# Six single-pass filler products taken out of the routing and the first expert of a decoder step

## What is computed

```python
def moe_ffn(x, router_w, router_b, w_gu, b_gu, w_down, b_down):
    logits = x2.astype(jnp.float32) @ router_w.astype(jnp.float32) + router_b.astype(jnp.float32)
    top_vals, top_idx = lax.top_k(logits, TOP_K)
    gates = jax.nn.softmax(top_vals, axis=-1).astype(x.dtype)
    ...
    def expert_block(args):
        xb, e = args
        gu = xb @ w_gu[e] + b_gu[e]
        gate = jnp.minimum(gu[:, :D_FF], SWIGLU_LIMIT)
        up = jnp.clip(gu[:, D_FF:], -SWIGLU_LIMIT, SWIGLU_LIMIT)
        h = (up + 1.0) * (gate * jax.nn.sigmoid(SWIGLU_ALPHA * gate))
        return h @ w_down[e] + b_down[e]
```

## Time and profile before

| | us |
|---|---|
| median of 3 runs | 1199.98 |
| lowest, highest | 1198.43, 1200.36 |
| profiled execution, its own time | 1200.14 |
| its span | 1198.4 |
| PE busy | 1145.1 (96%) |
| VectorE (DVE) busy | 520.2 (43%) |
| ScalarE (ACT) busy | 259.7 (22%) |
| mean bandwidth | 370 GB/s |
| mean granted clock of TensorE | 0.992 |

### The profile page before, as it was taken

The page is one execution under the profiler, slowest core; times in us unless marked ns, Lnnn a source line. Parts: engine busy times, 40 slices in busy tenths (PEclk is TensorE's granted clock), DMA queues, the critical chain, the costliest instruction groups (busy, mean ns, idle before and its releaser), DMA issues.

```text
span 1198.4 us, 13942 instructions
## 1 busy us (share of the span) xinstructions
PE 1145.1 (96%) x5682; PEld 555.7 (46%) x5682; DVE 520.2 (43%) x989; ACT 259.7 (22%) x405; POOL 3.3 (0%) x13
## 2 busy tenths in 40 slices
PE   9999999999999999999999989999999999999994
PEld 8999999663333333333333323333333333333331
DVE  6788888882332223333233322322222222222236
ACT  4655655411111111111111111111111111111112
POOL 1000000000000000000000000000000000000000
PEclk9999999999999999999999999999999999999997
DMA  9865844768999999999999999999999999999994
GB/s 229 259 209 173 246 141 129 296 263 325 417 429 427 427 427 428 428 427 428 428 428 427 427 428 428 427 427 428 427 428 427 427 428 428 427 428 428 427 424 157
DMA packets 93276, 443.77 MB, mean 370 GB/s; under 512 B 7848, under 2 KB 65336, under 8 KB 67998
## 3 DMA queue, kind: packets, MB, share of 16 engines
q1 hardware_dynamic: 93038, 442.41, 91.4%
q10 hardware_dynamic: 176, 0.48, 0.1%
HBM read 441.34 MB, written 1.53 MB: 370 GB/s over the span
## 4 chain that ended last, share of the span: by engine, by line
PE 61%; DMA 29%; DVE 6%; ACT 2%; issue 1%; DVEq 0%; SPq 0%; ACTq 0%
DMA ring<-in_w_gu 24%; PE PS L914 21%; PE PS L954 14%; PE PS L705 10%; PE PS L822 6%; DMA ring<-in_w_down 3%; PE PS L844 3%; PE PS L726 2%; DVE w_lo L1060 1%; PE PS L830 1%; DVE tiles L1103 1%; PE PS L837 1%; PE PS L736 1%; PE PS L994 1%; PE PS L877 1%
## 5 line engine op out<-in xcount | busy, mean ns | idle before, releaser
L914 PE MATMUL PS<-ring,mid 128*64 128x512 f32 x1920 | 423.1, 594 | 25.1 <-DMA ring<-in_w_gu 24.6
L914 PEld LDWEIGHTS PS<-ring,mid 128*64 128x64 f32 x1920 | 135.3, 137 | 306.2 <-issue 254.2
L954 PE MATMUL PS<-ring,mid 128*64 128x512 f32 x960 | 213.1, 595 | 0.0
L1382 DVE TENSOR_SCALAR PS<-PS 128x512 f32<-128x512 f32 x30 | 21.0, 699 | 359.0 <-PE PS L914 359.0
L705 PE MATMUL PS<-x_hi,w_hi 128*128 128x320 f32 x448 | 141.2, 315 | 1.4 <-ACT tiles L523 0.6
L705 PE MATMUL PS<-x_lo,w_hi 128*128 128x320 f32 x448 | 139.0, 310 | 0.0
L705 PE MATMUL PS<-x_hi,w_lo 128*128 128x320 f32 x448 | 138.9, 310 | 0.0
L1364 DVE TENSOR_TENSOR ys<-PS,ys 64x512 fp32r<-64x512 f32 x64 | 44.1, 689 | 193.8 <-ACT ys L610 185.6
L954 PEld LDWEIGHTS PS<-ring,mid 128*64 128x64 f32 x960 | 66.1, 137 | 130.2 <-issue 130.0
L1103 DVE SCALAR_TENSOR_TENSOR x_tok<-PS,gate,x_tok 128x1024 f32<-128x1024 f32 (+1 forms) x93 | 115.1, 1276 | 21.0 <-PE PS L844 21.0
L601 ACT ACTIVATE mid<-PS 128x512 f32<-128x512 f32 x30 | 17.9, 597 | 424.7 <-DVE PS L1382 424.7
(11 more groups left out here) (241 smaller groups left out, 751.2 us busy)
## 6 DMA issues: line engine op xcount, KB each, us to landing
ring<-in_w_gu SPq DMA_DIRECT2D x125, 2048.0 KB, 40.3
ring<-in_w_down SPq DMA_DIRECT2D x62, 2048.0 KB, 38.8
raw<-in_w_in SPq DMA_DIRECT2D x56, 512.0 KB, 5.7
ring<-in_w_gu SPq DMA_DIRECT2D x6, 1024.0 KB, 7.9
ring<-in_w_out SPq DMA_DIRECT2D x4, 1024.0 KB, 5.3
ring<-in_w_down SPq DMA_DIRECT2D x4, 1024.0 KB, 41.5
x_tok<-in_x_prompt SPq DMA_DIRECT2D x2, 512.0 KB, 5.0
out<-x SPq DMA_DIRECT2D x2, 512.0 KB, 2.7
```

The costliest lines, as they stand in the source:

```text
L914: last = mm(PS[64 * a:64 * a + 64, b, :], xgT[:, 2 * (u % 2) + j, u // 2, :], w[:, o:o + HALF], start=False, stop=(u == 3 and j == 1))
L954: last = mm(PS[64 * a:64 * a + 64, XB, :], hT[:, j, u, :], w[:, j * D + a * HALF:j * D + (a + 1) * HALF], start=(u == 0 and j == 0), stop= ...
L1382: dve.tensor_scalar(gm, gm, LIMIT, None, ALU.min).then_inc(gm_ok, 1)
```

## The change

The six calls' products are removed, and with them the function that issued them. Everything else is as it was: the same waits in the same order, the same banks, the same transfers.

```diff
@@ -653,11 +653,6 @@
             mm = pe.matmul
 
-            def keep_warm(n, bank):
-
-                for _ in range(n):
-                    mm(PS[:, bank, :], ones_r[:, :], bias4[:, 0, :], start=True, stop=True)
-
             def keep_busy(n, bank):
@@ -801,7 +796,6 @@
             last.then_inc(so_turned, 1)
-            keep_warm(1, 1)
 
             pe.wait_ge(mask_ok, 1)
@@ -811,7 +805,6 @@
             last.then_inc(cnt_done, 1)
-            keep_warm(3, 1)
             pe.wait_ge(so_ok, 1)
@@ -901,7 +894,6 @@
                     turn_x(xg_sb, tx_done)
-                    keep_warm(2, 7)
                 pe.wait_ge(xgT_ok, 2 * it + rows_in(i))
```

## The result

| | before, us | changed, us |
|---|---|---|
| median of 14 runs | 1199.57 | 1201.07 |
| lowest, highest | 1198.43, 1200.61 | 1199.77, 1206.00 |
| profiled execution, its span | 1200.14, 1198.4 | 1201.13, 1199.4 |

The account below looks back on a forecast made before the run. The end was taken to hang on the weights' DMA stream, whose start waits for the first freed slots. 1200.14 - 0.09 + 1.41 = 1201.46; against the median, 0.16 lower, 1201.3 us; range 1198.3 to 1203.5.

Parts of the forecast that it names:

- The bound: Whole kernel: the end is that of the weights' DMA stream plus a short tail; TensorE waits for weights from about 650 us.
- Shifts the end by that microsecond: Between router and 296 us: each microsecond TensorE loses or gains shifts the whole stream and the end equally.
- One lost after 650 us would cost nothing: Late experts: TensorE already waits for weights there, so a microsecond it loses costs 0.
- The direct part: Routing: time gained by removing six filler products, apart from the clock; -0.09 us, far bound -1.6 us.
- Gain: 0.09 us, not 0.78: Three fillers ahead of the gather: it also needs VectorE's one-hot matrix, so it starts at about 266.72 instead of 266.81.
- the other two places: Fillers ahead of the mask product and ahead of the expert's first products: hidden in waits, gain 0 each.
- The price of +1.41: Gather at the low clock: 4.35 us instead of 2.94, as seen at 715 us; all behind it follows.
- So a long wait lowers the clock, and so does a stretch of narrow work: TensorE's clock rule, read from falls at 11.3, 714.5 and 1185.5 us; applied to 2.5 us of routing without fillers.
- case B: Rival, chance 0.27: the clock holds in the routing and the fillers did nothing; time 1199.9 us.
- Its variant: Routing: the clock falls even before the change in some executions; the two medians then differ by less than 1.3.
- C: Rival, chance 0.14: early fall by about 265, two low stretches over gather, bias products, transposes; 2.8 us lost, time 1202.7.
- D: Rival, chance 0.03: the gather waited for the fillers and all are laid bare; 1.6 us faster, 1198.4.

Follow-up runs that it names:

- the early and the late twelve: Kernel before plus twelve 512-column products laid bare ahead of expert 0 (1202.06 us, ratio 1.0026) or of expert 8 (1199.60 us, ratio 1.0001).
- halves: Kernel before with each of the six ring slots that expert 0 frees given back in two halves: 1199.41 us against 1200.00, ratio 0.9995.
- upper group: Slow runs of the changed kernel, fillers removed: three of 14 at 1204.3 to 1206.0 us, then five of 11 at 1203.65 to 1205.89.
- narrow fillers: Kernel before with its six fillers of 512 columns replaced by sixteen of 32 columns: 1201.62 us, ratio 1.0016.
- the changed kernel again: The kernel without fillers, run once more with no edit: 1201.28 us against 1199.81 for the kernel before, ratio 1.0025.
- the third place alone: Changed kernel with only the two fillers between the gathered tokens' transposes and the wait for their copy back: 1200.80 us, ratio 1.0013.

## Why the prediction was right

**The bound.** Right, and shown by the early and the late twelve: the earlier trace rows were read correctly as a DMA stream whose start is tied to the first slots that the first expert frees. "Shifts the end by that microsecond" held within noise: 2.97 us more ahead of the first issue gave 2.55, and the stretch from the first issue to the end of the span lies between 921.9 and 924.3 us in all fourteen profiles. The two longest of the kernels without halves, 923.6 and 924.3, have their excess at the uneven end of the stream. "One lost after 650 us would cost nothing" has support too: in four profiles the clock was low for 10.2 us near 720 us, and three of these have 922.3 to 922.8 us from the first issue to the end, as others have. For a gain the sentence was not borne out: 1.7 us earlier gave only 0.6, as the restarted stream moved less at first.

**The direct part.** "Gain: 0.09 us, not 0.78" was right in refusing the chain's 0.78, and wrong in the 0.09. The gather starts 0.15 us behind the one-hot matrix with and without the fillers; I had set 0.05 by another pair of instructions. The gain is 0. For the other two places 0 was right: the mask products and the expert's first products start when they did.

**The clock.** The mechanism is the predicted one: a fall close to the gather, which the gather pays for. "I take the clock to fall once, at some moment between 264.5 and 268" was right: 267.2, 266.0, 267.5 and 267.3 us in the four profiles of the changed kernel in which it fell; in the fifth it held. The price of +1.41 was a little low: measured 4.59 - 2.94 = 1.65, since the gather at 715 us began when the clock had already been low for 0.5 us, and caught less of the stretch. The sum would have been +1.65 for an execution with one low stretch; the medians give +1.50, against a forecast of +1.3. That 1201.3 comes so close to 1201.07 is in part luck: the median of before was 0.4 us too high with its three runs, which made up for a gain that isn't there (0.09) and for the low price (0.24).

"So a long wait lowers the clock, and so does a stretch of narrow work" was too firm. The wait of 2.86 us ahead of the gather near 715 us is in all fourteen profiles, and the clock fell there in ten of them; at the start it also fell in ten of fourteen. What TensorE did before made a fall possible, and did not settle it. And the waits of 0.67 and 0.22 us that case B counts to the stretch up to 263 us lie behind it, at 264.5 and 271.7.

**The fillers' places.** The prediction took the six as one. The runs show that the three ahead of the gather are enough (0.9999).

**The rivals.** B (the clock holds) is real in single executions, in one of the five profiles of the changed kernel, but not in the median, and it can't be told from one profile. Its variant, a fall in the kernel before too, was in none of the six profiles with the three fillers in place. C named the right mechanism, more than one low stretch over gather, bias products and transposes, and the wrong trigger and size. I had put it down to an early fall, by about 265, at 2.8 us. In the profile that shows it the fall came late, at 267.5, and the clock stayed low for 10.2 us, not 6.8, at 4.2 us. I had given it 0.14; 3 of 14 runs and then 5 of 11 were in the upper group. None of these eight was profiled; the long stretch was seen in a further execution, the one of 1205.50 us, and in the one with narrow fillers of 1205.59. The median, which the forecast was about, stays in the lower group as long as the share is under a half, and 5 of 11 is close to that. D (fillers laid bare) is out.

## What to carry to other kernels

A filler that hides in a wait cost nothing here and may hold the clock for what follows, so before one is taken out, look at the granted clock and at which dense piece stands next behind the wait; the three fillers right ahead of it were enough here, and sixteen narrow ones did not help by the ratio. Price a lost microsecond by what waits for it, not by busy shares: ahead of a stream of transfers that couldn't start it cost nearly in full here (2.55 of 2.97 us), and inside a stretch of 100% busy TensorE next to nothing (0.09). And where the clock is at stake, look at all runs, not the median alone: here the change cost 1.5 us in the median, but some 4 us or more in 8 of 25 executions. One profile can't show such a thing: the same kernel had its clock low for 3.4 us in three executions, for 10.2 in a fourth and not at all in a fifth.

## What the runs showed of the hardware that was not expected

- Low stretches of very different length grew out of nearly the same start. In one execution of the changed kernel the clock fell at 267.3 and was back at 270.7, in another it fell at 267.5 and was back at 277.7, with instructions that started within 0.06 us of each other up to the gather. In the second execution the fall that comes near 720 us was long as well (granted clock 0.57 from 720 to 730 and 0.92 from 730 to 740). The two don't always go together: in two other profiles (the changed kernel again, and the third place alone) the routing's low stretch lasted 3.4 us and the one near 720 us lasted 10.2. Why was not settled.
- The wait of 2.86 us near 715 us is in all fourteen profiles. In ten of them the clock fell there, and in four it stayed at 1.00.
- In the one profile of it, sixteen products of 32 columns did not hold the clock where six or more of 512 did in five, though the profile shows the engine about as busy.
- The clock fell in only some executions of the same program, and at moments that differed by up to 0.8 us relative to the mask product (1.9 to 2.7 us behind it).
- With the stream just restarted, DMA moves less: in its first 10 us it moved 392 GB/s in the kernel before (276.5 to 286.5), 391 in the changed one (277.7 to 287.7) and 355 in the one with halves (274.3 to 284.3), against 428 in the steady part.
- The end of the stream is uneven. In the execution of 1205.50 us a single DMA engine's share (0.08 and 0.06) was left from 1183 to 1185 us, and the last down unit landed 894.1 us behind the first issue in place of 892.2.
